# Two attention loops: scores two steps ahead, copies shared by two engines, one mask product a head

## The reference

```python
def softmax_attention(q, k, v):
    s = jnp.einsum('bqhd,bkhd->bhqk', q, k).astype(jnp.float32) * MLA_SCALE
    p = jax.nn.softmax(s, axis=-1).astype(v.dtype)
    return jnp.einsum('bhqk,bkhd->bqhd', p, v)
...
        logits = jnp.einsum('bhqd,bhkd->bhqk', qi, k).astype(jnp.float32) * scale
        logits = logits + di[..., :, None] - dcum[..., None, :]
        logits = jnp.where(kpos[None, :] <= qpos[:, None], logits, -jnp.inf)
        p = jax.nn.softmax(logits, axis=-1)
        return jnp.einsum('bhqk,bhkd->bhqd', p.astype(v.dtype), v)
```

## Time and profile before

| what | us |
|---|---|
| median of 3 runs | 1286.98 (1286.17 to 1289.56) |
| the profiled execution | 1292.35 |
| its span, first to last instruction | 1290.5 |
| latent loop, first scores to last values | 39.50 (181.28 to 220.78) |
| FoX loop, first scores to last values | 42.25 (1006.50 to 1048.75) |

### The profile page before, as it was taken

How to read it: one execution, slowest core, us unless ns; L and a number is a source line. 1 busy time by engine, 2 the same in 40 slices (tenths; PEclk the granted TensorE clock), 3 DMA queues, 4 the chain that set the end, 5 groups by cost and what they waited for, 6 DMA issues and landing times.

```text
span 1290.5 us, 18186 instructions
## 1 busy us (share of the span) xinstructions
PE 1174.6 (91%) x7080; PEld 1010.3 (78%) x7080; DVE 834.4 (65%) x882; ACT 586.2 (45%) x838; POOL 219.2 (17%) x167
## 2 busy tenths in 40 slices
PE   4899988789999998888989999997989888999997
PEld 1588656669999886687869999886767776999986
DVE  3564457577667777788865448687688758544434
ACT  5433443336666446334355444245444526544433
POOL 1000600102555201020001322200102000132210
PEclk8999999799999998899989999998989979999999
DMA  9674433054655895965854568885695424555550
GB/s 347 256 257 172 150 131 137 3 196 132 194 180 182 306 351 191 374 225 212 305 199 145 183 195 303 317 309 183 227 323 183 144 85 131 164 178 181 194 193 36
DMA packets 124383, 263.69 MB, mean 204 GB/s; under 512 B 8313, under 2 KB 76481, under 8 KB 114081
## 3 DMA queue, kind: packets, MB, share of 16 engines
q1 hardware_dynamic: 121265, 252.46, 56.4%
q0 software_dynamic: 2768, 8.28, 2.1%
q10 hardware_dynamic: 288, 2.10, 0.4%
HBM read 261.76 MB, written 1.05 MB: 204 GB/s over the span
## 4 chain that ended last, share of the span: by engine, by line
PE 69%; DVE 16%; issue 7%; ACT 6%; DMA 3%; SPq 0%; DVEq 0%; ACTq 0%
PE ps L1601 19%; PE ps L1602 19%; PE ps L1603 19%; DVE acc L566 4%; ACT wh L1150 3%; DVE wl L554 2%; DMA au<-in_ada_w_dram 1%; PE ps L1679 1%; PE ps L1830 1%; PE ps L1626 1%; DVE hraw L672 1%; DVE x L695 1%; PE ps L1860 1%; PE ps L1844 1%; DVE xn L693 1%
## 5 line engine op out<-in xcount | busy, mean ns | idle before, releaser
L554 DVE TENSOR_TENSOR wl<-raw,wh 128x2048 fp32r<-128x2048 f32 (+1 forms) x154 | 350.5, 2277 | 301.7 <-ACT wh L1150 301.5
L1150 ACT ACTIVATE wh<-raw 128x2048 fp32r<-128x2048 f32 (+1 forms) x154 | 291.8, 1896 | 372.0 <-PE ps L1603 366.7
L1601 PE MATMUL ps<-hh,wh 128*128 128x256 f32 (+1 forms) x1192 | 338.6, 284 | 10.4 <-DVE wl L554 5.4
L1602 PE MATMUL ps<-hl,wh 128*128 128x256 f32 (+1 forms) x1192 | 337.6, 283 | 0.0
L1603 PE MATMUL ps<-hh,wl 128*128 128x256 f32 (+1 forms) x1192 | 337.2, 283 | 0.0
L1601 PEld LDWEIGHTS ps<-hh,wh 128*128 128x128 f32 (+1 forms) x1192 | 226.7, 190 | 14.1 <-issue 5.8
L1603 PEld LDWEIGHTS ps<-hh,wl 128*128 128x128 f32 (+1 forms) x1192 | 226.7, 190 | 0.2
L1602 PEld LDWEIGHTS ps<-hl,wh 128*128 128x128 f32 (+1 forms) x1192 | 226.7, 190 | 0.2
L566 DVE SCALAR_TENSOR_TENSOR acc<-au,cs,acc 128x2048 f32<-128x2048 f32 x72 | 172.8, 2400 | 5.4 <-DMA au<-in_ada_w_dram 5.2
L1601 PE MATMUL ps<-wh,hh 128*128 128x512 f32 (+1 forms) x352 | 141.5, 402 | 19.6 <-DVE wl L554 6.3
L2263 POOL TENSOR_TENSOR gl<-hid,gh 128x256 f32 (+1 forms) x66 | 93.3, 1414 | 325.6 <-ACT gh L1455 325.6
(11 more groups left out here) (314 smaller groups left out, 1436.5 us busy)
## 6 DMA issues: line engine op xcount, KB each, us to landing
au<-in_ada_w_dram SPq DMA_DIRECT2D x48, 1024.0 KB, 6.9
raw<-in_ffn_w_gu_dram SPq DMA_DIRECT2D x88, 512.0 KB, 4.6
raw<-in_w_up_dram SPq DMA_DIRECT2D x44, 512.0 KB, 4.7
raw<-in_ffn_w_down_dram SPq DMA_DIRECT2D x44, 512.0 KB, 4.5
au<-in_w_ada_dram SPq DMA_DIRECT2D x16, 1024.0 KB, 5.6
raw<-in_a_w_in_dram SPq DMA_DIRECT2D x32, 512.0 KB, 5.7
raw<-in_w_down_dram SPq DMA_DIRECT2D x22, 512.0 KB, 4.4
raw<-in_w_in_dram SPq DMA_DIRECT2D x16, 512.0 KB, 4.5
```

Of the source, the lines that this page charges most:

```text
L554: nc.vector.tensor_tensor(wl[:, s % 2, 0:n], raw[:, u % RAW, 0:n], wh[:, s % 2, 0:n].bitcast(F32), ALU.subtract).then_inc(lo_done, 1)
L1150: nc.scalar.activation(wh[:, s % 2, 0:n], raw[:, u % RAW, 0:n], ACT.Copy).then_inc(hi_done, 1)
L1601: nc.tensor.matmul(to, lh, rh, start=start, stop=False, skip_group_check=True)
L1602: nc.tensor.matmul(to, lh, rl, start=False, stop=False, skip_group_check=True)
```

## The change

In both loops the scores are issued two steps ahead instead of one. For that they go round four banks: 4, 5, 2, 3 in the latent loop (its values need only 0 and 1), and in FoX by a table: 4, 5, 1, 3 while banks 1 and 3 hold no values yet, then 4 and 5, with heads 12 and 13 in banks 0 and 2, which VectorE has emptied by then. It empties them in the loop: at head 8 it divides the first eight heads' values (`fox_half(0)`), and behind the loop only the other eight, then both gates one after the other.

The turned probabilities of even steps are still copied by VectorE, those of odd steps by ScalarE, which does the copy of step `it-1` behind the exponential of step `it`. In FoX the two mask products of a head become one: a float32r product of `ident_r` with `neg_r`, read twice by a stride of 0, onto both diagonal blocks at once (2x128 columns, 128 apart). The two float32r operands are made by POOL before its rotation of the retention rows. The constant `pick`, which nothing used, is dropped (256 KB less to load). The wait of the turns of the retention keys on the last copy is dropped too.

```diff
+        SCORE_BANKS = (4, 5, 2, 3)
+        FOX_BANKS = (4, 5, 1, 3, 4, 5, 1, 3, 4, 5, 4, 5, 0, 2, 4, 5)
...
             head_max(0)
+            head_max(1)
             for it in range(2 * MLA_H):
-                if it + 1 < 2 * MLA_H:
-                    head_max(it + 1)
-                dve.wait_ge(p_turned, it + 1)
-                if it >= 2:
-                    dve.wait_ge(pv_done, it - 1)
-                nc.vector.tensor_copy(prob_t[:, it % 2, :], ps[:, 6 + it % 2, :]).then_inc(pt_ready, 1)
+                if it + 2 < 2 * MLA_H:
+                    head_max(it + 2)
+                if it % 2 == 0:
+                    dve.wait_ge(p_turned, it + 1)
+                    if it >= 2:
+                        dve.wait_ge(pv_done, it - 1)
+                    nc.vector.tensor_copy(prob_t[:, 0, :], ps[:, 6, :]).then_inc(pt_ready, 1)
                 if it % 4 == 3:
                     ada_part(17 + it // 4)
...
+            def fox_half(half):
+
+                dve.wait_ge(fp_ready, 16 * (half + 1))
+                link(nc.vector.reciprocal(prec[:, 16 * half:16 * half + 16], psumr[:, 16 * half:16 * half + 16]))
+                dve.wait_ge(fpv_done, 8 * (half + 1))
+                for t in range(NT):
...
+                if half == 0:
+                    ins.then_inc(fo_first, 1)
+                else:
+                    link(ins)
...
+                if h == 8:
+                    fox_half(0)
                 if h % 3 == 1 and h < 15:
                     ada_part(72 + h // 3)
...
+            fox_half(1)
...
             for it in range(2 * MLA_H):
                 act.wait_ge(max_ready, it + 1)
                 if it >= 2:
                     act.wait_ge(p_turned, it - 1)
...
+                if it % 2 == 0 and it >= 2:
+                    copy_probs(it - 1)
+            copy_probs(2 * MLA_H - 1)
...
             scores(0)
+            scores(1)
             for it in range(2 * MLA_H):
-                if it + 1 < 2 * MLA_H:
-                    scores(it + 1)
+                if it + 2 < 2 * MLA_H:
+                    scores(it + 2)
                 turn_probs(it)
                 if it >= 1:
                     values(it - 1)
...
             def fox_scores(h):
-                if h >= 2:
-                    pe.wait_ge(fp_ready, 2 * (h - 1))
-                bank = 4 + h % 2
+                bank = fox_bank(h)
+                held = [j for j in range(h) if fox_bank(j) == bank]
+                if held:
+                    pe.wait_ge(fp_ready, 2 * held[-1] + 2)
+                if bank in (0, 2):
+                    pe.wait_ge(fo_first, 1)
...
-                nc.tensor.matmul(ps[:, bank, 0:P], ident, neg, start=False, stop=True, skip_group_check=True)
...
-                nc.tensor.matmul(ps[:, bank, 2 * P:3 * P], ident, neg, start=False, stop=True,
+                own = ps[:, bank, :].rearrange("p (a c) -> p a c", a=2)[:, :, 0:P]
+                nc.tensor.matmul(own, ident_r[:, :], bcast(neg_r[:, :], 1, 2), start=False, stop=True,
                                  skip_group_check=True).then_inc(fs_done, 1)
...
+            nc.gpsimd.tensor_copy(ident_r[:, :], ident).then_inc(neg_ready, 1)
+            nc.gpsimd.tensor_copy(neg_r[:, :], neg).then_inc(neg_ready, 1)
```

More of the change, by code:

```diff
@@ L1099, in fox_max @@
                 dve.wait_ge(fs_done, h + 1)
-                nc.vector.tensor_reduce(nmax[:, 2 * h:2 * h + 1], ps[:, 4 + h % 2, 0:P], AX.X, ALU.max, negate=True)
-                nc.vector.tensor_reduce(nmax[:, 2 * h + 1:2 * h + 2], ps[:, 4 + h % 2, P:3 * P], AX.X, ALU.max,
+                bank = fox_bank(h)
+                nc.vector.tensor_reduce(nmax[:, 2 * h:2 * h + 1], ps[:, bank, 0:P], AX.X, ALU.max, negate=True)
+                nc.vector.tensor_reduce(nmax[:, 2 * h + 1:2 * h + 2], ps[:, bank, P:3 * P], AX.X, ALU.max,
                                         negate=True).then_inc(fm_ready, 1)
-            fox_max(0)
-            for h in range(FH):
-                if h + 1 < FH:
-                    fox_max(h + 1)
-                dve.wait_ge(fp_turned, h + 1)
-                if h >= 2:
-                    dve.wait_ge(fpv_done, h - 1)
-                nc.vector.tensor_copy(prob_ft[:, h % 2, :], ps[:, 6 + h % 2, 0:384]).then_inc(fpt_ready, 1)
-                if h % 3 == 1 and h < 15:
-                    ada_part(72 + h // 3)
-            dve.wait_ge(fp_ready, 2 * FH)
-            link(nc.vector.reciprocal(prec[:, :], psumr[:, :]))
-            dve.wait_ge(fpv_done, FH)
-            dve.wait_ge(evac, EVACS + 16)
-            for t in range(NT):
-                for half in range(2):
+            def fox_half(half):
[3 more added lines that the diff above has]
+                for t in range(NT):
                     sums = prec[:, 16 * half + t:16 * half + 16:2]
@@ L1124, in _ @@
                                                   bcast(sums, 2, FD), ALU.mult)
-                link(ins)
+                if half == 0:
+                    ins.then_inc(fo_first, 1)
+                else:
+                    link(ins)
+            fox_max(0)
+            fox_max(1)
+            for h in range(FH):
+                if h + 2 < FH:
+                    fox_max(h + 2)
+                if h % 2 == 0:
+                    dve.wait_ge(fp_turned, h + 1)
+                    if h >= 2:
+                        dve.wait_ge(fpv_done, h - 1)
+                    nc.vector.tensor_copy(prob_ft[:, 0, :], ps[:, 6, 0:384]).then_inc(fpt_ready, 1)
+                if h == 8:
+                    fox_half(0)
+                if h % 3 == 1 and h < 15:
+                    ada_part(72 + h // 3)
+            fox_half(1)
+            dve.wait_ge(evac, EVACS + 16)
+            dve.wait_ge(fo_first, 1)
+            for t in range(NT):
                 nc.vector.tensor_tensor(o_f[:, t, :], o_f[:, t, :], sg[:, t, :], ALU.mult).then_inc(xn_ready, 1)
@@ L1365, in _, with copy_probs @@
             nc.scalar.activation(lg[:, 1, :], lg[:, 3, :], ACT.Exp).then_inc(lg_exp, 1)
+            def copy_probs(it):
+                act.wait_ge(p_turned, it + 1)
+                if it >= 2:
+                    act.wait_ge(pv_done, it - 1)
+                nc.scalar.activation(prob_t[:, 1, :], ps[:, 7, :], ACT.Copy).then_inc(pt_act, 1)
             for it in range(2 * MLA_H):
@@ L1575, in _, with fox_copy @@
             turned_heads(qt_f, 8)
+            def fox_copy(h):
+                act.wait_ge(fp_turned, h + 1)
+                if h >= 2:
+                    act.wait_ge(fpv_done, h - 1)
+                nc.scalar.activation(prob_ft[:, 1, :], ps[:, 7, 0:384], ACT.Copy).then_inc(fpt_act, 1)
             for h in range(FH):
@@ L1581, in _ @@
                     lo_, hi_ = (0, P) if t == 0 else (P, 3 * P)
-                    nc.scalar.activation(prob_f[:, h % 2, lo_:hi_], ps[:, 4 + h % 2, lo_:hi_], ACT.Exp,
+                    nc.scalar.activation(prob_f[:, h % 2, lo_:hi_], ps[:, fox_bank(h), lo_:hi_], ACT.Exp,
                                          bias=nmax[:, 2 * h + t:2 * h + t + 1],
                                          accum_out=psumr[:, 2 * h + t:2 * h + t + 1]).then_inc(fp_ready, 1)
+                if h % 2 == 0 and h >= 2:
+                    fox_copy(h - 1)
+            fox_copy(FH - 1)
             evac_high(N_FOX, hh, (0, 1))
```

41 lines of the change are left out of this document (24 added, 17 removed).

## The result

The changed kernel takes 1276.43 us (median of 4 runs, 1272.75 to 1277.59); the kernel before, run beside it, 1286.76 (4 runs, 1286.17 to 1289.56). The ratio is 0.9897, with a 95% interval of 0.9864 to 0.9929. The medians differ by 10.3 us, where 14.6 were forecast. The forecast was 1272.4 in a range of 1267.5 to 1279.5, so the time lies within the range, 4 us on the slow side and just above the forecast's own range (1268.5 to 1276). The profiled execution took 1277.41 us, its span is 1275.6; against the 1290.5 of before that is 14.9 us, almost exactly the sum of 14.6 in the prediction.

A forecast was written before the change was run, and what follows sets the result against it. TensorE, busy 91%, was taken as the bound, so savings count where it waits or its stream shortens. 4.1 + 10.0 + 0.8 - 0.3 = 14.6 us off 1286.98 gave 1272.4; range 1267.5 to 1279.5, own range 1268.5 to 1276.

The forecast's parts named there:

- Latent loop: Latent attention loop: scores two steps ahead remove TensorE's waits at every fourth step; 4.1 us saved, possibly 2.5.
- The free 0.4 us: Latent loop: after a modulation part, VectorE's even copy is done at 4.2 us and asked for at 4.6.
- The step behind it: Decays behind the latent loop: load of diff lands 2.83 us after sending, so the chain moves forward whole.
- rival 2: Modulation weights don't keep up in FoX, 3 us late at each of four parts; 1278 to 1284 us, chance 0.05.
- FoX: FoX loop: 1.78 us a head instead of 2.10, ending at 1038.7 against 1048.75; 10.0 us saved.
- the four waits: FoX: late copies after parts at heads 1 and 7 (0.3 each), division 0.3, head 14's copy 1.4; together 2.3 us.
- The 4.9 us "by waits that go": FoX loop: share of the 10.0 us saved put down to vanishing waits; the mask gives the other 5.1.
- Tail: Behind FoX: half the division done in the loop, so gate row 1 is turned sooner; 0.8 us saved.
- POOL's copies: Ahead of the retention rotations: two 128x128 copies, about 0.8 us, delay POOL; 0.3 us lost, bounds 0 and 1.0.
- rival 1: A new wait replaces the old: late copies, or mask form costing 0.43; 1277.4 to 1280.4 us, chance 0.17.
- rival 4: The gain doesn't reach the end, taken up by a later DMA-bound stage; 1284 to 1288 us, chance 0.04.
- Rival 3: Both loops lose the clock, each microsecond of stream at 1.2 GHz costing one more; 1302 us at half, chance 0.03.

The follow-up runs named there:

- again: The changed kernel once more, nothing altered; 1273.68 to 1280.86 us in 5 runs, ratio 0.9912 to the kernel before.
- latent: The kernel before with only the latent loop's part of the change; 1289.01 us, ratio 0.9994.
- fox: The kernel before with only the FoX part of the change, mask included; 1279.29 us, ratio 0.9907.
- vcopies: The changed kernel with all copies of the turned probabilities on VectorE again, scores still two ahead; 1279.81 us in one execution.
- diffwait: The changed kernel, but SyncE holds one transfer of modulation weights until diff has landed; 1273.04 to 1276.85 us, ratio 0.9897.
- oneahead: The changed kernel with scores and maxima only one step ahead in both loops; 1297.27 us in one execution.
- oneahead2: The same kernel as oneahead, timed in 8 runs; 1299.68 us, ratio 1.0072 to the kernel before.
- fill: oneahead plus four surplus products, read by nobody, ahead of FoX's first turn; 1285.32 us, ratio 0.9963 to the kernel before.
- best: The changed kernel with diff loaded early, FoX's last modulation part behind head 14's copy, POOL's two copies behind its rotations; 1272.6 us, ratio 0.9850.

## Why the prediction was right, and where it wasn't

**Latent loop: right.** Its length was to be 35.3 us and is 35.34. The free 0.4 us held at all four parts; no row of TensorE in the loop has an idle note. The first turn begins 2.69 us after the first scores, as before, where 0.13 more had been put down. A copy costs ScalarE 0.60, not 0.55:

```profile
200.84 0.60 ACT L1400 ACTIVATE prob_t<-ps 128x512 f32<-128x512 f32 x1 [0.46 <-PE ps L1902]
```

**The step behind it: wrong.** "This chain hangs on the last values alone, so it moves forward whole." The issue of the load does hang on them alone; its duration doesn't. It hangs on what is under way on the DMA engines, and that is released by the end of VectorE's last part. It ended 1.1 us behind the last values before (219.54 + 2.34 against 220.78) and ends 0.1 us ahead of them now (211.51 + 2.34 against 213.95), while the load is issued 0.3 us behind them in both. The prediction weighed the transfers in FoX (rival 2), and for the claim that nothing else can be late it named the DMA share of 0.00 behind FoX, which is another place; here it took over the 2.83 us of the earlier trace rows without asking what stood behind them. The order of VectorE's instructions was there to be read: VectorE copies nothing behind step 14, so the part of step 15 starts as soon as that copy is done (211.51), before the last values. Cost 2.44 us, and five more kernels agree: 5.29, 5.16 and 5.09 us for the load where the weights go first (changed kernel, again, latent), 3.09, 2.93 and 2.92 where they don't (fox, vcopies, diffwait). Where the weights go 0.7 us ahead instead of 0.36, it is 4.87, 4.64 and 4.70 (oneahead, oneahead2, fill).

**FoX: right, 0.6 short.** 9.4 us saved where 10.0 were forecast. Head 1.77 (forecast 1.78), mask slot 0.12 as taken. Of the four waits three came as counted: turn to values takes 0.58 instead of 0.33 behind the parts of heads 1 and 7 (forecast 0.3 each), and 1.71 instead of 0.33 at head 14 (1.4). The fourth was mis-sized: around the division of the first half the turns are 2.94 apart instead of 1.77, of which 0.25 are the late copy and some 0.9 the division (forecast 0.3). The 4.9 us "by waits that go" hold 1.1 that are no waits: the end of the loop before ran at half clock, and the count of the new loop took the full clock throughout.

**Tail: right.** 0.74 saved, 0.8 forecast, at the half clock it was reckoned with (0.52).

**POOL's copies: open.** From its first instruction to the last product of its rotations POOL takes 19.96 us before (133.85 to 153.81), 20.75 with the two copies ahead (133.50 to 154.25), and 19.91 in best, which has them behind. So they push the rotations back by 0.8 us. How much of it reaches TensorE (0.3 put down) lies within the scatter of the stretch ahead of the latent loop (178.2 to 183.7 us over all kernels) and was not settled. A kernel that moves them (best) starts its latent loop at 180.83, which tells nothing.

**Sum.** 14.6 forecast, 11.85 by the stages: 2.4 of the difference is the load, 0.6 FoX, the rest are small terms that went the other way (POOL's 0.3). The 14.9 between the two profiles owed 3 us to stretches that the change doesn't touch; the profiled execution of before stood 5.6 us above the median of its runs, that of after 1.0.

**Rivals.** A new wait in place of the old one (rival 1) did come true in kind, at a place that rival 1 did not name. The weights kept up (rival 2): no row of either loop waits for a transfer. The gain does reach the end (rival 4 doesn't hold): the rest of the program takes 233.75 us where it took 234.25. Rival 3, the lost clock, didn't happen, but oneahead2 shows that its mechanism is real at exactly this place. Its price, a microsecond for each of the stream, was too high for FoX: from its first turn on, oneahead's loop has 51.8 us of stream at half clock, which would be 25.9 at the full one, while fill's has 36.5 with its waits. So some 10.6 us of waits vanish under the longer stream, and 15.3 are left to pay. The reason against it was weak, though. "1.00 and 0.97 before, with longer gaps" compares means over loops. The 0.97 was itself the sign: the loop before lost the clock behind its last wait, for 2.5 us at its end. And how close the entry of the loop is to losing it (waits of 1.21 before and 1.09 after keep it, idle time that begins 0.7 to 0.8 us sooner in oneahead doesn't) the prediction didn't ask. The rule that the prediction weighed, of the Trainium skill's "TensorE: Matmul & The Clock Gate", section "A second HAM failure mode: psum-queue depth-cycling", is not seen here: with four banks in turn the clock is 1.00 in both loops. oneahead and fill go round the same banks, and one loses the clock at the entry and the other keeps it, so the banks are not what decides.

## What to carry to other kernels

A stage made shorter moves the DMA requests that its instructions release: for each load that a later stage waits for, look at what is sent just ahead of it, on whatever queue, before and after. Send a small load that is needed at a fixed point early, as soon as a buffer can be found for it. Take stage lengths from one profile, but a total never: the loops at full clock repeat to 0.01 us, stages with a load or a change of clock in them to 0.1 to 0.3 (12.76 and 12.64 for the changed kernel and again, 42.21 and 41.93 for the FoX loop of before in two kernels). At this kernel's scatter of 0.3%, 2 us are only to be shown stage by stage.

## What was not expected of the hardware

Idle time at the entry of a loop can halve TensorE's clock for all of it. In oneahead2 TensorE was busy without a gap from the first turn on and had the 1.2 GHz level to the end, 30 to 40 us after the wait as 10 to 20 us after it:

```profile
1022.00:1032.00 10.00, 10.00 (x43) 9.46 (x42) 4.40 (x9) 3.50 (x14) 0.00 (x0) 0.50 0.27 89
1042.00:1052.00 10.00, 10.00 (x43) 9.46 (x42) 4.58 (x8) 3.50 (x14) 0.00 (x0) 0.50 0.22 71
```

The Trainium skill, "TensorE: Matmul & The Clock Gate", section "What's actually happening", says that activity releases the throttle. Here a stream that the profile shows as busy without a gap didn't release it in the 50 us up to the loop's end. It came back behind the loop, in the output product (products over 512 columns): 1.4 us after the first of them in oneahead2 (1070.74 to 1072.1), 1.6 in oneahead. Why the loop's stream of small products keeps the full clock once it has it (fill, 1.00 with TensorE idle a tenth of the time) and doesn't win it back was not tried, nor whether the two waits just ahead of the loop (1.70 and 0.78 us) have a part in the fall. One wait alone doesn't tell: 1.70 us cost nothing here, 1.53 cost the clock in fill.

The second is the size of the DMA effect: 1 MB that starts 0.36 us earlier makes a load of 256 KB take 5.1 to 5.3 us instead of 2.9, while the DMA share in the 12.75 us behind the latent loop is 0.29. During the load itself it is 0.69 (the changed kernel, by stretch):

```profile
213.95:226.70 12.75, 6.34 (x40) 5.34 (x38) 8.39 (x15) 7.13 (x12) 1.99 (x3) 0.99 0.29 103
214.24:219.53 5.29, 4.34 (x31) 3.90 (x30) 1.25 (x4) 3.04 (x6) 0.56 (x1) 1.00 0.69 248
```

A low mean share over a stage does not say that a single load in it finds the engines free.
